# Scores of the second and third key groups: one head's two groups of q stacked in one stationary operand, k as block diagonals

## What is computed

```python
DILATED_GROUPS = ((128, 1), (512, 4), (2048, 16))
...
def dilated_mixture_attention(q, k, v):
    B, S = q.shape[:2]
    cos, sin = rope_tables(S)
    q = apply_partial_rope(q, cos, sin)
    k = apply_partial_rope(k, cos, sin)
    outs, lses = [], []
    for g, (window, dilation) in enumerate(DILATED_GROUPS):
        hs = slice(g * HEADS_PER_GROUP, (g + 1) * HEADS_PER_GROUP)
        o, lse = dilated_window_attention(q[:, :, hs], k[:, :, hs], v[:, :, hs], window, dilation)
        outs.append(o)
        lses.append(lse)
    alpha = jax.nn.softmax(jnp.stack(lses, axis=0), axis=0)
    o = jnp.sum(alpha[..., None] * jnp.stack(outs, axis=0), axis=0)
    return o.reshape(B, S, ATTN_OUT_WIDTH).astype(v.dtype)
```

## Time and profile before

| | us |
|---|---|
| median of 3 runs | 1863.39 |
| lowest, highest run | 1862.91, 1864.31 |
| the profiled execution | 1862.57 |
| its span, first to last instruction | 1860.8 |
| PE busy in the span | 1845.2 |

### The profile page before, as it was taken

One profiled execution on the slowest core, in us unless ns is written; L12 is line 12 of the kernel. 1 busy time (PEld: TensorE's weight loads), 2 busy tenths in 40 slices (PEclk: granted clock), 3 DMA queues, 4 the chain that ended last, 5 costly groups with the idle time before them and its releaser, 6 DMA issues.

```text
span 1860.8 us, 27165 instructions
## 1 busy us (share of the span) xinstructions
PE 1845.2 (99%) x10801; PEld 1627.8 (87%) x10807; DVE 1324.6 (71%) x1778; ACT 879.1 (47%) x1170; POOL 73.3 (4%) x96
## 2 busy tenths in 40 slices
PE   9999999999999999999999999999999999999997
PEld 7998998888889989989998888888888888888886
DVE  8875887888778888856888745463647776666666
ACT  6652664435355535634653332423336644444445
POOL 0000000120000000000000000000000000000000
PEclk9999999999999999999999999999999999999999
DMA  6744763462317526654753222122221222212213
GB/s 213 184 122 125 197 171 101 176 151 70 118 46 210 147 91 175 164 160 123 195 153 117 91 91 91 68 93 79 99 88 48 91 88 72 91 70 88 90 68 91
DMA packets 51506, 218.86 MB, mean 118 GB/s; under 512 B 5856, under 2 KB 8448, under 8 KB 39888
## 3 DMA queue, kind: packets, MB, share of 16 engines
q1 hardware_dynamic: 38960, 180.90, 28.9%
q0 software_dynamic: 12016, 36.04, 9.8%
q10 hardware_dynamic: 432, 0.56, 0.1%
HBM read 205.41 MB, written 5.77 MB: 113 GB/s over the span
## 4 chain that ended last, share of the span: by engine, by line
PE 73%; DVE 5%; ACT 2%; issue 1%; DMA 0%; DVEq 0%; POOL 0%; ACTq 0%
PE acc L2449 16%; PE acc L2451 16%; PE acc L2450 16%; PE acc L2456 4%; PE acc L2455 4%; PE acc L2457 4%; PE att L2450 2%; PE att L2451 2%; PE att L2449 2%; DVE w_lo L1377 1%; PE att L2455 1%; PE att L2457 1%; PE att L2456 1%; PE acc L2717 1%; PE acc L2692 1%
## 5 line engine op out<-in xcount | busy, mean ns | idle before, releaser
L1377 DVE TENSOR_TENSOR w_lo<-raw,w_hi 128x2048 fp32r<-128x2048 f32 (+1 forms) x120 | 271.0, 2258 | 69.8 <-ACT w_hi L668 68.9
L668 ACT ACTIVATE w_hi<-raw 128x2048 fp32r<-128x2048 f32 (+1 forms) x120 | 226.1, 1884 | 120.5 <-PE acc L2451 106.3
L2449 PE MATMUL acc<-x_hi,w_hi 128*128 128x512 f32 x712 | 280.9, 394 | 0.6 <-DVE x_lo L1440 0.3
L2451 PE MATMUL acc<-x_hi,w_lo 128*128 128x512 f32 x712 | 277.4, 390 | 0.0
L2450 PE MATMUL acc<-x_lo,w_hi 128*128 128x512 f32 x712 | 277.3, 389 | 0.0
L2449 PEld LDWEIGHTS acc<-x_hi,w_hi 128*128 128x128 f32 x712 | 133.7, 188 | 30.5 <-issue 2.9
L2450 PEld LDWEIGHTS acc<-x_lo,w_hi 128*128 128x128 f32 x712 | 133.7, 188 | 29.0 <-issue 1.6
L2451 PEld LDWEIGHTS acc<-x_hi,w_lo 128*128 128x128 f32 x712 | 133.7, 188 | 28.0
L2455 PE MATMUL acc<-xt_hi,w_hi 128*128 128x256 f32 x516 | 144.5, 280 | 0.0
L2457 PE MATMUL acc<-xt_hi,w_lo 128*128 128x256 f32 x516 | 144.3, 280 | 0.0
L2456 PE MATMUL acc<-xt_lo,w_hi 128*128 128x256 f32 x516 | 144.3, 280 | 0.0
(11 more groups left out here) (487 smaller groups left out, 4663.5 us busy)
## 6 DMA issues: line engine op xcount, KB each, us to landing
raw<-in_ret_head SPq DMA_DIRECT2D x24, 1024.0 KB, 4.8
raw<-in_ffn_down SPq DMA_DIRECT2D x32, 704.0 KB, 4.2
raw_c<-in_ffn_seven SPq DMA_DIRECT2D x37, 512.0 KB, 5.2
raw<-in_ffn_seven SPq DMA_DIRECT2D x33, 512.0 KB, 4.8
raw<-in_ffn_seven POOLq DMA_DIRECT2D x33, 512.0 KB, 7.6
raw<-in_ffn_seven SPq DMA_DIRECT2D x37, 256.0 KB, 4.6
raw<-in_ret_out SPq DMA_DIRECT2D x8, 1024.0 KB, 4.7
raw<-in_sb_v SPq DMA_DIRECT2D x8, 1024.0 KB, 4.7
```

The lines of the kernel that those rows point to most:

```text
L668: nc.scalar.activation(w_hi[:, slot, at:at + cols], raw[:, slot, 0:cols], ACT.Copy).then_inc(w_hi_ready, 1)
L1377: tt(w_lo[:, slot, at:at + cols], raw[:, slot, 0:cols], w_hi[:, slot, at:at + cols].bitcast(F32), ALU.subtract).then_inc(w_ready, 1)
L2449: mm(dst, still[0], move[0], start=first, stop=False)
L2451: return mm(dst, still[1], move[0], start=False, stop=last)
```

## The change

The columns of the weights are regrouped on the host, so that the second and third projections of q (and of k) no longer hold one key group of both heads, but one head of both key groups: rows 0 to 63 the second key group, rows 64 to 127 the third. q then needs no copies: its parts `q_hi`, `q_lo` are the stationary operands as they are. k is written in two instructions of 64 rows into two column blocks (a block diagonal; the other halves are zeroed once). A unit's six matmuls of 128 columns become three of 256 columns. `q_pair`, `q_head`, their eight DMAs and the waits on them go. DVE's two instructions on q become one, and its one on k becomes two, with a wait of DVE for the second; ACT's one on k becomes two. `first_score` waits for the second part of k's low part instead of the copies.

```diff
@@ memory
-            q_pair = sb("q_pair", [P, 2, TOK], F32R, under)
...
-                q_head = [sb(f"q_head{j}", [P, 2, N_GROUPS - 1, TOK], F32R, inner) for j in range(2)]
-                k_hi = sb("k_hi", [P, N_GROUPS - 1, TOK], F32R, inner)
-                k_lo = sb("k_lo", [P, N_GROUPS - 1, TOK], F32R, inner)
+                q_hi = sb("q_hi", [P, 2, TOK], F32R, inner)
+                q_lo = sb("q_lo", [P, 2, TOK], F32R, inner)
+                k_hi = sb("k_hi", [P, 2, 2, TOK], F32R, inner)
+                k_lo = sb("k_lo", [P, 2, 2, TOK], F32R, inner)
@@ POOL
-                nc.gpsimd.memset(q_head[j][rows, :, :, :].bitcast(F32), 0.0).then_inc(rest_clear, 1)
+                for part in (k_hi, k_lo):
+                    nc.gpsimd.memset(part[rows, :, j, :].bitcast(F32), 0.0).then_inc(rest_clear, 1)
...
-                for g in range(N_GROUPS - 1):
-                    pool.wait_ge(pair_low_ready, (N_GROUPS - 1) * a + g + 1)
-                    for j in range(2):
-                        pool.dma_start(q_head[j][own[j], :, g, :], q_pair[own[j], :, :]).then_inc(head_landed, 16)
@@ ACT, rope_done
                 if g and o:
-                    ins = nc.scalar.activation(k_hi[:, g - 1, :], t(o), ACT.Copy, scale=QK_SCALE[o])
+                    for i, rows in enumerate(head_rows):
+                        ins = nc.scalar.activation(k_hi[rows, g - 1, i, :], t(o)[rows, :], ACT.Copy, scale=QK_SCALE[o])
                 elif g:
-                    if pairs.k:
-                        act.wait_ge(head_landed, 2 * 16 * pairs.k)
-                    pairs.next()
-                    ins = nc.scalar.activation(q_pair[:, 0, :], t(o), ACT.Copy, scale=QK_SCALE[o])
+                    ins = nc.scalar.activation(q_hi[:, g - 1, :], t(o), ACT.Copy, scale=QK_SCALE[o])
@@ DVE, rope_done
                 if g and o:
-                    stt(k_lo[:, g - 1, :], t(o), QK_SCALE[o], k_hi[:, g - 1, :].bitcast(F32), ALU.mult, ALU.subtract).then_inc(op_ready, 1)
+                    for i, rows in enumerate(head_rows):
+                        stt(k_lo[rows, g - 1, i, :], t(o)[rows, :], QK_SCALE[o], k_hi[rows, g - 1, i, :].bitcast(F32),
+                            ALU.mult, ALU.subtract).then_inc(half_low_ready if i else op_ready, 1)
+                    dve.wait_ge(half_low_ready, lows.next())
                 elif g:
-                    for j, cols in enumerate((EARLY, LATE)):
-                        stt(q_pair[:, 1, cols], t(o)[:, cols], QK_SCALE[o], q_pair[:, 0, cols].bitcast(F32),
-                            ALU.mult, ALU.subtract).then_inc(pair_low_ready if j else op_ready, 1)
-                    dve.wait_ge(pair_low_ready, lows.next())
+                    stt(q_lo[:, g - 1, :], t(o), QK_SCALE[o], q_hi[:, g - 1, :].bitcast(F32), ALU.mult, ALU.subtract).then_inc(op_ready, 1)
@@ PE, scores and first_score
-                for g in range(N_GROUPS - 1):
-                    last = passes(narrow[:, P * g:P * (g + 1)], [q_head[head][:, i, g, plain[r]] for i in range(2)],
-                                  (k_hi[:, g, plain[r]], k_lo[:, g, plain[r]]), False, g == N_GROUPS - 2)
+                last = passes(narrow[:, 0:2 * P], (q_hi[:, head, plain[r]], q_lo[:, head, plain[r]]),
+                              (k_hi[:, head, :, plain[r]], k_lo[:, head, :, plain[r]]), False, True)
...
-                pe.wait_ge(rest_clear, 4)
+                pe.wait_ge(rest_clear, 6)
                 pe.wait_ge(both_landed, 4 * 16 * (a + 1))
-                pe.wait_ge(head_landed, 2 * (N_GROUPS - 1) * 16 * (a + 1))
+                pe.wait_ge(half_low_ready, (N_GROUPS - 1) * (a + 1))
@@ host, order of the weights' columns
-    w["mix_qk"] = np.stack([np.stack([np.stack([cols[2 * g + c], cols[qc + 2 * g + c]], 1)
-                                      for g in range(N_GROUPS)]) for c in range(2)]).reshape(2, N_GROUPS, P, SLAB)
+
+    def one_head(first, c, j):
+        return np.concatenate([cols[first + 2 * g + c][..., HEAD * j:HEAD * (j + 1)] for g in range(1, N_GROUPS)], -1)
+
+    w["mix_qk"] = np.stack([np.stack([np.stack([cols[c], cols[qc + c]], 1)]
+                                     + [np.stack([one_head(0, c, j), one_head(qc, c, j)], 1) for j in range(2)])
+                            for c in range(2)]).reshape(2, N_GROUPS, P, SLAB)
```

More of the change, by code:

```diff
@@ L413, in block_kernel @@
         both_landed = sem("both_landed")
-        pair_low_ready = sem("pair_low_ready")
-        head_landed = sem("head_landed")
+        half_low_ready = sem("half_low_ready")
         park_landed = sem("park_landed")
@@ L657, in _ @@
             n, s, u, b = Count(), Count(), Count(), Count()
-            val, turn, pairs = Count(), Count(), Count()
+            val, turn = Count(), Count()
             def prep(cols=SLAB, seg=0):
```

## The result

The changed kernel takes 1868.36 us (median of 11 runs, 1866.53 to 1869.27), the kernel before 1862.90 (11 runs beside them, 1862.43 to 1864.31): a ratio of 1.0027, with a 95% interval of 1.0019 to 1.0035. Its profiled execution took 1868.63, with a span of 1866.8, 6.0 more than before.

The account below looks back on a forecast made before the run. PE is 99% busy, but attend's units were held by a loop through ACT and DVE, and the first values by their serial chain. 2.6 + 1.85 = +4.45 us on 1862.57 gave 1867.0, plus 0.8 to the median: 1867.8 (range 1865.0 to 1869.4).

Parts of the forecast that it names:

- Scores worth nothing: In attend's units, PE saves 0.27 us each, 4.3 in all, but the loop hides it; PE's wait becomes 0.33.
- k: Two 64-row pieces cost ACT +0.64 us and DVE +0.69 (or +0.80), making the chain 1.33 (or 1.44) later per k.
- First pair: +2.6: DVE's slab split, hence PE's first values, comes 2.6 us late, and what is queued behind stays so until the loop.
- the clock: Rival: PE's granted clock halves at the first values, adding 0 to 10.9 us, 1867.8 to 1878.7; chance 0.05.
- Second pair: +1.85: End of the second qk and start of attend(1): the DVE and ACT path 1.94 us late, less 0.1, gives +1.85.
- PE's path at the start: Rival: shorter scores count until the units' loop begins, both pairs together +2.35 us, 1865.7; chance 0.14.
- POOL and DMA at nothing: Eight copies leave POOL's queue, zeroing comes in four pieces, fetches follow DVE's splits: all costed at nothing.
- Sum: Both pairs together, 2.6 + 1.85 = +4.45 us, with nothing behind the attention taking it back.

Follow-up runs that it names:

- b_half_scores: The kernel before, with the third key group's three 128-column score matmuls left out of each unit: 1862.47 us, 0.34 below before.
- b_k_two: The kernel before, with only k of the second and third group split by ACT and DVE in two 64-row pieces: 1869.76 us, 6.95 above before.
- a_k_one: The changed kernel, with k back in one 128-row instruction each of ACT and DVE (block diagonal given up): 1862.24 us, 0.57 below before.
- a_fill: The changed kernel, with the low part of k's second piece made later, where DVE waits for ACT anyway: 1863.90 us, 0.61 above before.
- a_reorder: The changed kernel, with DVE's sum over a unit's bank moved between the two low parts of the next unit's weights: 1867.23 us, 3.94 above before.
- a_spare: The changed kernel, with ten spare 512-column matmuls ahead of the slab's wait at the first values: 1867.10 us, 4.29 above before.
- a_spare5: The changed kernel, with five spare 512-column matmuls ahead of the slab's wait at the first values: 1867.07 us, 4.07 above before.

## Why the prediction came out as it did

The sign and the mechanism were right. The size was nearly right, with two errors in opposite directions: a sum 1.0 too small and a starting median 0.5 too high. So that 1867.8 came within 0.6 is in part luck.

- **Scores worth nothing: right.** Turns are 2.87 apart as before, PE's wait ahead of each grew from 0.06 to 0.42 - 0.12 = 0.30 (0.33 forecast), and b_half_scores shows that no PE time in the scores counts in this order of DVE's work. The new form costs about what was taken: three at 0.12, 0.36 instead of 0.34, so 0.61 - 0.36 = 0.25 us a unit less for PE (0.27 forecast). The reason was right too: with the loop of the earlier trace rows shortened, the saved time appears in the distances.
- **k: right.** ACT 1.27 and DVE 1.40 for the two pieces (1.27 and 1.41 forecast). The Trainium skill (ScalarE: Activation LUTs, section Rules for kernel authors) prices an ACT instruction by a fixed part and a part per element, and has no part for rows; the trace agrees in that 64 rows cost 0.63 and 128 rows 0.63.
- **First pair: +2.6 right at the first `values`, wrong behind it.** PE started 2.79 late, of which 2.55 is its wait. The step that failed is the sentence that what is queued behind stays 2.6 late until the loop: it became 3.67. ACT and DVE, which showed no wait for PE that the shift would not move along, got one: ACT waits 0.71 for PE at 431.13. Missing was the clock. It stood among the rivals, with a chance of 0.05 and a price between 0 and 10.9; it happened, with a price of 0.9, and the measured 1868.36 lies in its range (1867.8 to 1878.7) as well as in the forecast's. The mistake was to treat it as another outcome. It is a consequence of the forecast's own wait, and belongs in the sum as a term. The Trainium skill (TensorE: Matmul & The Clock Gate, Part 1: The HAM clock gate) says that an idle PE loses the higher level; the granted clock of 0.50 behind the pause agrees.
- **Second pair: +1.85, measured 522.63 - 516.91 - 3.67 = 2.05.** Against the first pair's lateness at unit 7, 460.80 - 457.12 = 3.68, the turn came 502.98 - 497.92 - 3.68 = 1.38 late (1.30 forecast), DVE's last low part began at 506.50 where 500.81 + 1.94 + 3.68 = 506.43 was forecast, PE waited 1.84 (1.7). Only the first score was off: PE starts it 508.38 - 507.90 = 0.48 behind DVE's end, and I had put 0.21.
- **PE's path at the start: a part of that rival is true.** It holds in the kernels whose clock fell. There PE's path, some 1.3 us slower (2.9 us of matmuls 0.21 apart instead of 0.113), became the later one, and on it shorter scores count: b_k_two, with the same pauses and the same half clock but the old scores, is 0.42 later than the changed kernel at unit 2 of the first pair, and 0.5 more in the second. In the first pair the trace shows the step: the scores of units 0 and 1 stand on PE ahead of ACT's part of v, and with the old ones this part begins 0.43 later (431.56 against 431.13), after 0.44 more waiting (timeline of ACT, b_k_two):

```profile
431.56 0.84 ACT L936 ACTIVATE va<-acc,r_tok 128x256 fp32r<-128x256 f32 x2 [1.15 <-PE acc L2456]
```

For the second pair this was not tested by itself. Behind the attention b_k_two takes 1331.2 us (1869.1 - 537.86), 1.4 more than the changed kernel. Of this, 0.9 is one wait: at 583.25 ACT has waited 1.94 for a fetch of weights (`raw<-in_mix_seven`), and PE waits 0.91 for ACT at 584.63, which in the changed kernel it doesn't. The rest stays open. The profiled execution is also the slowest of b_k_two's five (1870.9; median 1869.76), and its ratio's interval overlaps the changed kernel's.

- **POOL and DMA at nothing: borne out.** a_k_one has the changed kernel's POOL queue and is not slower than before; b_k_two has the old one and is slow.
- **Sum.** Forecast +4.45, measured 5.73 at unit 7 of the second pair, 6.0 on the spans and 5.5 on the medians. Nothing behind the attention takes it back: 1866.8 - 536.96 = 1329.8, before 1860.8 - 531.23 = 1329.6. I also started from a median of three runs, 1863.39, that was 0.5 above that of eleven, 1862.90; on that one the same sum gives 1867.35. So the sum itself was 1.0 us short on the medians, about what the clock cost. On the trace, up to unit 7 of the second pair, it was 1.28 short: 0.19 at the first `values` (inside the scatter of that start), 0.88 by the clock, 0.20 in the second pair.

## What to carry to other kernels

Before a saving on the busiest engine is counted, look for the loop that sets the distance between repeats; if two limits lie within a few per cent, price both edits together, because each alone can give next to nothing (here -0.34 and -0.41, but -2.15 together). Here an instruction on half the rows cost as much as on all of them (ACT 0.63, DVE 0.69 to 0.70), so count instructions on the serial chain between ACT and DVE and not bytes; a piece that is not needed at once goes into the next wait (a_fill: 4.9 of 5.5 us back). And where a new wait stops PE for some microseconds, put a fall of its clock into the sum as a term, from nothing up to the slower matmuls behind the wait; here it was 0.9.

## What the runs showed of the hardware that was not expected

- A pause of PE in a stream that ran at 2.4 GHz was followed by the 1.2 GHz level in some places and not in others. It was behind pauses of 2.55 (changed), 2.73 (b_k_two), 2.58 (a_reorder) and 1.95 (a_spare), and it was not behind 2.00 (b_k_two, second pair), 1.93 (changed) and 1.37 (a_spare5). The granted clock stayed at 1.00 from 500 to 512 us in b_k_two, so the length of a pause alone does not tell. In the changed kernel the clock fell while PE still waited; in a_reorder only 1.4 after PE had resumed (busy time and granted clock by stretch; PE resumes at 410.31):

```profile
410.00:412.00 2.00, 1.69 (x13) 1.69 (x14) 1.89 (x4) 1.01 (x1) 0.00 (x0) 0.93 0.35 97
412.00:414.00 2.00, 2.00 (x12) 2.00 (x11) 1.93 (x3) 0.00 (x0) 0.00 (x0) 0.50 0.09 34
```

- Its price depends on what comes behind: 0.9 us where DVE and ACT follow PE closely, nothing where PE had another wait ahead (a_spare's second pair). Ten or five useless matmuls in the pause of the first pair took this loss away, and PE would have waited there anyway.
